# Two heads at a time in the three attentions of a small diffusion network: scores on different rows, value products on different columns of the array

## What is computed

```python
def diff_attend(q, k, v, lam):
    s = jnp.einsum('bqhmd,bkhmd->bhmqk', q, k).astype(jnp.float32) * (DIFF_QK ** -0.5)
    p = jax.nn.softmax(s, axis=-1)
    a = p[:, :, 0] - lam * p[:, :, 1]
    return jnp.einsum('bhqk,bkhd->bqhd', a.astype(v.dtype), v)
```

## Time and profile before

| | us |
|---|---|
| median of three runs | 2183.61 |
| the profiled execution | 2185.96 |
| its span | 2184.2 |
| TensorE matmuls busy | 2094.0 (96%), 18040 instructions |
| weight loads busy | 1987.5 (91%) |
| VectorE busy | 1436.1 (66%) |
| ScalarE busy | 1085.3 (50%) |
| GpSimd busy | 480.6 (22%) |
| mean DMA rate | 162 GB/s |
| mean granted clock | 0.98 of full |

### The profile page before, as it was taken

One profiled execution on the slowest core, in us unless ns is written; L12 is line 12 of the kernel. 1 busy time (PEld: TensorE's weight loads), 2 busy tenths in 40 slices (PEclk: granted clock), 3 DMA queues, 4 the chain that ended last, 5 costly groups with the idle time before them and its releaser, 6 DMA issues.

```text
span 2184.2 us, 42595 instructions
## 1 busy us (share of the span) xinstructions
PE 2094.0 (96%) x18040; PEld 1987.5 (91%) x18040; DVE 1436.1 (66%) x2728; ACT 1085.3 (50%) x1879; POOL 480.6 (22%) x226
## 2 busy tenths in 40 slices
PE   7999999999998989999889988999999999999998
PEld 5977999999998789999778888999999999999998
DVE  3445478877785666666663656589388897666665
ACT  5333352232335455546433445555577776555564
POOL 1201100000011120001211341188766662000000
PEclk9999999999998999999999999999999999999999
DMA  7245345566663345654221234555444445555553
GB/s 275 104 139 180 117 164 185 172 223 227 207 222 118 115 145 205 225 196 134 83 70 58 78 109 161 175 193 190 168 140 146 150 146 174 194 193 194 194 194 134
DMA packets 97278, 354.90 MB, mean 162 GB/s; under 512 B 10688, under 2 KB 11712, under 8 KB 96704
## 3 DMA queue, kind: packets, MB, share of 16 engines
q1 hardware_dynamic: 97088, 352.18, 47.9%
HBM read 351.09 MB, written 1.05 MB: 161 GB/s over the span
## 4 chain that ended last, share of the span: by engine, by line
PE 86%; DVE 5%; ACT 3%; issue 3%; DMA 2%; POOL 2%; SPq 0%; ACTq 0%; DVEq 0%; POOLq 0%
PE ps L79 82%; PE ps L84 3%; DVE TL L113 1%; PE ps L106 1%; ACT TH L157 1%; POOL TL L113 1%; DMA RAW<-in_wada 1%; ACT SQ L154 1%; DMA AW<-in_wada 1%; POOL SM L113 0%; ACT Hh L157 0%; DMA RAW<-in_wdn 0%; DVE ps L113 0%; DMA RAW<-in_wup 0%; DVE SQ L113 0%
## 5 line engine op out<-in xcount | busy, mean ns | idle before, releaser
L157 ACT ACTIVATE TH<-RAW 128x1024 fp32r<-128x1024 f32 (+1 forms) x515 | 539.8, 1049 | 281.8 <-PE ps L79 253.6
L113 DVE TENSOR_TENSOR TL<-RAW,TH 128x1024 fp32r<-128x1024 f32 (+1 forms) x343 | 424.5, 1238 | 238.1 <-ACT TH L157 237.2
L113 POOL TENSOR_TENSOR TL<-RAW,TH 128x1024 fp32r<-128x1024 f32 x172 | 413.2, 2405 | 507.2 <-ACT TH L157 481.2
L79 PE MATMUL ps<-Hh,TL 128*128 128x256 f32 x1920 | 450.3, 287 | 17.2 <-DVE TL L113 8.5
L79 PE MATMUL ps<-Hl,TH 128*128 128x256 f32 x1920 | 439.5, 281 | 0.0
L79 PE MATMUL ps<-Hh,TH 128*128 128x256 f32 x1920 | 439.4, 281 | 0.0
L79 PE MATMUL ps<-HXh,TL 128*128 128x256 f32 x1314 | 365.6, 282 | 7.0 <-POOL TL L113 3.1
L79 PEld LDWEIGHTS ps<-Hh,TL 128*128 128x128 f32 x1920 | 322.7, 192 | 42.9 <-issue 17.9
L79 PE MATMUL ps<-HXh,TH 128*128 128x256 f32 x1314 | 360.0, 278 | 0.0
L79 PE MATMUL ps<-HXl,TH 128*128 128x256 f32 x1314 | 359.9, 278 | 0.0
L79 PE MATMUL ps<-W,TH 128*128 128x256 f32 x2052 | 349.1, 276 | 0.0
(11 more groups left out here) (335 smaller groups left out, 3112.4 us busy)
## 6 DMA issues: line engine op xcount, KB each, us to landing
RAW<-in_ut SPq DMA_DIRECT2D x128, 512.0 KB, 3.3
RAW<-in_v SPq DMA_DIRECT2D x128, 512.0 KB, 3.3
RAW<-in_wup SPq DMA_DIRECT2D x88, 512.0 KB, 4.3
AV<-in_wada SPq DMA_DIRECT2D x80, 512.0 KB, 3.8
RAW<-in_win SPq DMA_DIRECT2D x74, 512.0 KB, 3.5
RAW<-in_wada SPq DMA_DIRECT2D x56, 512.0 KB, 3.6
RAW<-in_wdn SPq DMA_DIRECT2D x32, 512.0 KB, 4.4
RAW<-in_wout SPq DMA_DIRECT2D x24, 512.0 KB, 3.7
```

Of the source, the lines that this page charges most:

```text
L79: return self.e.matmul(out, lhs, rhs, start=first, stop=last, skip_group_check=skip)
L113: return DRY if self.e is None else self.e.tensor_tensor(out, a, b, op)
L157: return DRY if self.e is None else self.e.activation(out, a, ACT.Copy, **kw)
```

## The change

The units are put in such an order that neighbours are two heads of the same query block: in the layers `2 * j + hh` with `hh` innermost, in block 2 kv innermost. All loops go over pairs p of units 2p and 2p+1. The scores of a pair are issued together, in the layers on the four row tiles 0, 32, 64, 96, in block 2 on the row tiles 0 and 64. The value products of a pair alternate between the columns 0 to 63 and 64 to 127 and share one bank, and one copy (`keep`) takes both. The fifth head tile and the spread of head 3 move ahead of the loop of block 2, and the mLSTM's tiles one unit forward.

```diff
@@ weight_tiles, fill2, units_of, first_heads
-    for i in FILLS2[0:5]:
+    for i in FILLS2[0:6]:
...
-    return FILLS2[5 + u:6 + u]
+    return FILLS2[6 + u:7 + u]
...
-    return [(s, qb, h) for s in streams_of(l) for h in range(4) for qb in range(2)]
+    return [(s, qb, 2 * j + hh) for s in streams_of(l) for j in range(2) for qb in range(2) for hh in range(2)]
...
-    return n_units(l) - 3
+    return n_units(l) // 2 - 2
@@ TensorE, scores
-            def scores(n):
-                st, qb, hd = units[n]
-                j, r0 = hd // 2, 64 * (hd % 2)
+            def scores(p):
+
+                st, qb, hd = units[2 * p]
+                j = hd // 2
...
-                for mp in range(2):
-                    o = bank(("s", l, n, mp), A, "exp", l, n, mp)
-                    r = r0 + 32 * mp
-                    last = pe.mm_at(o[:, 0:cols], y.q[r:r + 32, j, 256 * st + 128 * qb:256 * st + 128 * qb + 128],
+                o = [bank(("s", l, n, mp), A, "exp", l, n, mp) for n in (2 * p, 2 * p + 1) for mp in range(2)]
+                for z in range(4):
+                    r = 32 * z
+                    last = pe.mm_at(o[z][:, 0:cols], y.q[r:r + 32, j, 256 * st + 128 * qb:256 * st + 128 * qb + 128],
                                     y.k[r:r + 32, j, k0:k0 + cols], (r, 0))
-                last.then_inc(*P.mark("s", l, n))
+                    if z % 2:
+                        last.then_inc(*P.mark("s", l, 2 * p + z // 2))
@@ TensorE, loop of the layers (new side)
+            for p in range(len(units) // 2):
+                st, qb, hd = units[2 * p]
+                two, nk = (2 * p, 2 * p + 1), 4 if st == 0 else 2
+                for n in two:
+                    pe.wait_ge(D, "att", l, n)
+                    o = bank(("turn", l, n), A, "attT", l, n)
+                    for c in range(nk):
+                        last = pe.turn(o[:, 128 * c:128 * c + 128], y.att[n % 2][:, 128 * c:128 * c + 128], eye)
+                    last.then_inc(*P.mark("turn", l, n))
+                if 2 * p + 2 < len(units):
+                    scores(p + 1)
+                for n in two:
+                    for what in fills_at(l, n):
+                        fill(what)
+                    ada("unit", l, n)
+                if p == first_heads(l):
+                    head_stats(0)
+                if p == first_heads(l) + 1:
+                    head_spread(0)
                 pe.wait_ge(A, "vd", l, 1)
-                pe.wait_ge(A, "attT", l, n)
-                o = bank(("o", l, n), D, "keep", l, n)
+                pe.wait_ge(A, "attT", l, 2 * p + 1)
+                o = bank(("o", l, p), D, "keep", l, p)
                 for c in range(nk):
                     tb = c + (0 if st == 0 else 2)
-                    last = pe.mm(o[r0:r0 + 64, 0:128], y.vd[:, tb, 64 * hd:64 * hd + 64],
-                                 y.attT[n % 2][:, 128 * c:128 * c + 128], c == 0, c == nk - 1)
-                last.then_inc(*P.mark("o", l, n))
+                    for hh in range(2):
+                        last = pe.mm_at(o[64 * hh:64 * hh + 64, 0:128], y.vd[:, tb, 64 * (hd + hh):64 * (hd + hh) + 64],
+                                        y.attT[hh][:, 128 * c:128 * c + 128], (0, 64 * hh), c == 0, c == nk - 1)
+                last.then_inc(*P.mark("o", l, p))
@@ VectorE, loop of the layers (new side)
+            for p in range(pairs):
+                two = 2 * p, 2 * p + 1
+                for n in two:
+                    if n + 2 < len(units):
+                        softmax(n + 2)
+                if p:
+                    keep(p - 1)
...
+                for n in two:
+                    for what in fills_at(l, n):
+                        fill(what)
+                    if n < len(units) - 1:
+                        ada("unit", l, n)
+                    if n + 2 < len(units):
+                        normal(n + 2)
@@ TensorE, block 2 (new side)
+        head_tile(4)
+        head_spread(3)
+        for p in range(8):
+            for n in (2 * p, 2 * p + 1):
+                pe.wait_ge(D, "att2", n)
...
+            if p < 7:
+                scores2(p + 1)
+            if p == 2:
                 for d in range(2):
                     recur5(d)
...
+            for n in (2 * p, 2 * p + 1):
+                if n + M_EARLY < 16:
+                    mlstm_tile(n + M_EARLY)
+                if n == 0:
+                    head_rope(3)
+                    head_stats(4)
+                elif n == 1:
+                    head_spread(4)
+                elif n == 3:
+                    head_rope(4)
+                ada("unit", 2, n)
```

More of the change, by code:

```diff
@@ L909, in tensor_program @@
                 win(16, 512, A, "tr", l, "vd", 0)
-                for j in range(2):
-                    scores(j)
+                scores(0)
                 win(17, 512, A, "tr", l, "vd", 1)
@@ L1108, in tensor_program @@
         head_stats(3)
-        scores2(1)
-        for n, (c, kv, qb) in enumerate(a_units):
-            pe.wait_ge(D, "att2", n)
-            o = bank(("turn2", n), A, "attT2", n)
-            for kc in range(4):
-                last = pe.turn(o[:, 128 * kc:128 * kc + 128], m.prob[n % 3][:, 128 * kc:128 * kc + 128], eye)
-            last.then_inc(*P.mark("turn2", n))
-            if n + 2 < 16:
-                scores2(n + 2)
-            if n == 4:
+        head_tile(4)
+        head_spread(3)
@@ L1142, in tensor_program @@
+            last.then_inc(*P.mark("o2", p))
         turn_rows(0, 4, (2, "vm", 3), D, "mv", 3)
@@ L1575, in scalar_program @@
             highs(at_tile["wout", l, 1])
-            stats(("o", l, 1), y.o[:, 1, 0:T], T, D, "keep", l, len(units) - 1)
+            stats(("o", l, 1), y.o[:, 1, 0:T], T, D, "keep", l, pairs - 1)
             mix_high(2)
@@ L2174, in mix_low @@
                     .then_inc(*D.mark("mix_low", l, k))
-            for n in range(len(units)):
-                if n + 2 < len(units):
-                    softmax(n + 2)
-                if n:
-                    keep(n - 1)
-                if n == len(units) - 1:
-                    lows(at_tile["wout", l, 0])
-                for what in fills_at(l, n):
-                    fill(what)
-                if n < len(units) - 1:
-                    ada("unit", l, n)
-                if n + 2 < len(units):
-                    normal(n + 2)
-                if n == first_heads(l):
+            pairs = len(units) // 2
+            for p in range(pairs):
+                two = 2 * p, 2 * p + 1
+                for n in two:
+                    if n + 2 < len(units):
+                        softmax(n + 2)
+                if p:
+                    keep(p - 1)
+                if p == pairs - 1:
+                    lows(at_tile["wout", l, 0])
+                for n in two:
+                    for what in fills_at(l, n):
+                        fill(what)
+                    if n < len(units) - 1:
+                        ada("unit", l, n)
+                    if n + 2 < len(units):
+                        normal(n + 2)
+                if p == first_heads(l):
                     head_above(0)
-                if n == first_heads(l) + 1:
+                if p == first_heads(l) + 1:
                     for k in MIX_ORDER[:4]:
@@ L2194, in vector_program @@
                     mix_d(0)
-            keep(len(units) - 1)
+            keep(pairs - 1)
             lows(at_tile["wout", l, 1])
@@ L2736, in gpsimd_program @@
             taken = [2 * what[1] + what[2] if what[0] == "gate" else 10 + what[1]
-                     for u in range(first_heads(l) + 2) for what in fills_at(l, u) if what[0] in ("four", "gate")]
+                     for u in range(2 * first_heads(l) + 2) for what in fills_at(l, u) if what[0] in ("four", "gate")]
             lows(at_tile["win", l, taken[-1]])
```

193 lines of the change are left out of this document (89 added, 104 removed).

## The result

The changed kernel takes 2213.94 us (median of four, 2207.93 to 2220.24), the kernel before 2185.64 in the same comparison. The ratio on record is 1.0121 (95% interval 1.0100 to 1.0142; the two medians by themselves give 1.0129). It is 1.2% slower, where I had forecast 2187, "no change that can be told", with an upper end of 2203. The profiled execution of after took 2220.24 us, the highest of its four.

The account below looks back on a forecast made before the run. TensorE was taken as the bound, with 86% of the span. The sum -39.6 + 23.4 + 13.2 + 3.1 + 4.6 - 1.3 = +3.4 us, added to the 2183.61 median, gave 2187 us, range 2173 to 2203.

Parts of the forecast that it names:

- The savings: TensorE in the attentions: paired value products 18.6 us, scores 19.0, fewer transpose switches 2.0; in all 39.6 us saved.
- Rival 3: A pair's value products don't run together on TensorE, giving 2206 us; chance 0.05.
- The bank: TensorE's next first fill waits for VectorE's copy to free a PSUM bank; 21.5 us in layers, 23.4 together.
- Second maps: In the layers, a pair's second map comes late from VectorE and TensorE waits: 13.2 us, ends 6 and 18.
- Block 2: Windowed attention: waits for GpSimd's tile and VectorE's recurrence and maps, net of old holes: cost 3.1 us before savings.
- The clock: In the layers, a little under three new TensorE holes bring half clock: 4.6 us, ends 0 and 25.
- rival 1: Slower, 2198 us: half clock follows many of 14 layer holes, 1.7 us each; chance 0.34.
- the spreads: Head spreads of both layers find their roots ready: 1.3 us saved.
- Rival 2: Faster, 2174 us: second-map waits don't add to bank waits, and block 2 gains its savings; chance 0.18.

Follow-up runs that it names:

- busy_holes: The changed kernel with extra unused TensorE matmuls filling its waits for the bank and for second maps in the layers: 2193.45 us, ratio 1.0050.
- layers_tail: The changed kernel with VectorE's copy ahead of softmaxes, both next maps between fills, and steps reordered at the layers' attention ends: 2166.40 us, ratio 0.9917.
- all_three: The whole change with layers_tail's edits, plus block 2's GpSimd tile and VectorE maps made earlier and its recurrence split: 2156.25 us, ratio 0.9874.
- keep_first: The changed kernel with VectorE's copy of the previous pair's value product ahead of the two softmaxes in both layers: 2182.23 us, ratio 0.9979.
- maps_only: The changed kernel with both maps of the next pair made between a round's fills in the layers, copy still behind softmaxes: 2200.02 us, ratio 1.0069.

## Why the prediction was wrong

**The savings, -39.6 us: right.** Value products of a pair 1.09 us (priced by the gMLP row), four score tiles 1.14. Rival 3 falls: by the rule that the Trainium skill gives (TensorE: Matmul & The Clock Gate, Part 3), weight loads overlap running matmuls only where row groups differ, and these don't; 16 matmuls on alternating column halves took the time of 8, so the measurement speaks against the rule for this case.

**The bank, 23.4 us: right.** The eight holes of the layers measured 3.17 and 2.10 us each (priced 3.23 and 2.15), in all 21.1, and the one of block 2 2.06 (priced 1.9), all ended by VectorE's copy.

**Second maps, 13.2 us: right in sum.** 1.63, 1.52, 2.68, 4.15 and 0.98 in layer 0 (11.0 for 9.5), 2.81 for 1.6 in layer 1's pair 0; the 2.1 in its pair 2 did not come. 13.8 us.

**Block 2, right.** The stage was to be 12.3 us shorter (17.3 saved, 5.0 of it lost) and is 10.5. GpSimd's tile cost 4.44 us (4.6), the recurrence 9.84 and 2.00 (7.7 and 2.6).

**The clock, 4.6 us: the step that failed.** Punished means here: followed by half clock. "I take a little under three as so punished" should have read all eight of the bank, which stood in or just ahead of half clock, and three of the six for second maps besides. In the layers the two stages give 14.1 and 8.7 us of slower work (the busy time after, less the busy time before without the work saved), 22.8 against 4.6, and busy_holes measured 19.8 of it directly. I had one hole of 2.9 us that was punished and one of 2.2 that was not the earlier trace rows and went by the second for eight holes, four of which were 3.2 us long, above the punished one. I also read both as too long: TensorE works 0.29 and 0.26 us within these windows, and the waits themselves are 2.64 and 1.96 us. And the price, "half clock for 3.4 us loses 1.7 at most", took every stretch for 3.4 us; of the eleven in or at the end of the two stages after, six lasted 6.8 us. The neighbourhood was written down too ("another of 1.1 to 2.9 within 6 us") and then not priced. With all fourteen of rival 1 at 1.7 us, 23.8, my own sum would have been 3.4 - 4.6 + 23.8, so 2206. Rival 1 is what happened, and its stated middle of 2198 counted too few holes. The rest, up to the measured 2213.94, is the next paragraph's and the 2 us by which the kernel before was slower in this comparison.

**Steps that were not priced: 6 us idle and their clock.** ScalarE's first output tile moved ahead of two copies in place of one (0.33 us of wait became 1.16, and 1.96 became 3.99), and GpSimd's bound in layer 1 (2.96 us, up to 6.5 with the clock). The second I had read and called equal; seven and six units would have shown in one line of arithmetic. It was a queue that a step is moved past, and the rule to count each such queue was applied to block 2 and not here.

The terms for the layers now close: -22.4 (work) + 21.1 (banks) + 13.8 (maps) + 22.8 (clock) + 5.8 (ends) - 2.4 (the spreads, and a wait of 1.2 in layer 1 that the new order hides) = 38.7, measured 38.6. That they close tests the holes alone: the clock's 22.8 is what TensorE's busy time is above the work that should be left, so it closes by itself, and its test is busy_holes.

**Rival 2** was wrong as put: the waits did add. But its claim that VectorE has the time was true: in another order most of both kinds of wait go, and layers_tail with 2166.40 lies below the 2174 it gave.

## What to carry to other kernels

When two units become one pair, each other engine's queue wants pairing in the order of what TensorE needs next, which here was: first the copy that frees a bank, then what starts a chain, then both results, and only then work on the side. A hole in TensorE is not priced by its length alone: here 38 us of added idle time in the layers' attentions brought 23 us of slow matmuls, so that the waits cost 1.6 times their length. And where a loop's bounds are rewritten, the range on every engine is worth counting out.

## What the runs showed of the hardware

VectorE can stand still for a GpSimd operation. Of the 2.81 us at layer 1's first pair, in all runs with the layers' new order, 2.1 come from an operation on 128 x 1 numbers (the kernel before has the same stall, and a wait of only 1.19 us from it, since its second map was wanted later). VectorE, twice the same operation, then GpSimd, all of after:

```profile
752.47 0.16 DVE L113 TENSOR_TENSOR l1st<-l1st,SM 128x1 f32<-128x1 f32 x1
...
753.93 2.26 DVE L113 TENSOR_TENSOR l1st<-l1st,SM 128x1 f32<-128x1 f32 x1
```

```profile
751.31 2.54 POOL L113 TENSOR_TENSOR l1st<-l1st,SM 128x8 f32<-128x8 f32 x1 [12.98 <-DVE l1st L119]
753.83 2.34 POOL L113 TENSOR_TENSOR TL<-RAW,TH 128x1024 fp32r<-128x1024 f32 x1
```

The slow one starts 0.10 us behind GpSimd's low part and ends 0.02 us behind it (756.19 and 756.17); the other takes 0.16 us. In all_three one of the recurrence's operations does the same, 2.67 us where its like takes 0.68. The Trainium skill has the rule (SBUF — State Buffer, "SBUF: two separate sides"): a VectorE operation with two inputs from SBUF and a GpSimd operation that reads SBUF share a port pair, and whichever starts first holds it for its whole duration. The stall behind the low part agrees. So does a control: a VectorE operation with one input from PSUM that starts within such a low part is not held up (two of 0.7 us each).

```profile
1616.22 1.29 DVE L113 TENSOR_TENSOR W<-ps,T 128x512 fp32r<-128x512 f32 x2 [1.48 <-PE ps L79]
```

```profile
1615.31 2.37 POOL L113 TENSOR_TENSOR TL<-RAW,TH 128x1024 fp32r<-128x1024 f32 x1 [6.84 <-ACT TH L157]
```

That holds 124 times in after. One row differs: the 0.16 us at 752.47 lie within a GpSimd operation too, from 751.31 to 753.85, on 128 x 8 numbers read from SBUF, and nothing waits. So the pair is not held through every GpSimd operation as recorded; why not this one, no run shows. In block 2 of the kernel before, 2.0 of the first hole's 4.80 us are such a stall as well (VectorE's 128 x 1 operation on mst at 1065.54 takes 2.18 us, its like 0.15). A low part on GpSimd at the wrong moment thus costs the critical path 2 us; no run moved layer 1's away.

The second surprise is how short a hole the clock fell behind. In the layers of after, keep_first, maps_only and busy_holes TensorE has 21 holes of 2.7 to 4.2 us up to the last value product; at 19 of them the clock falls to 1.2 GHz for 3.4 or 6.8 us, within the hole's last 1.4 us or up to 1.1 us behind it. The two that are not (2.70 us in maps_only, 2.96 in busy_holes) lie at the same place, GpSimd's tile in layer 1, where in after 2.96 us were punished. So the same hole can be punished or not, and from these runs only its likelihood can be priced.
